# The last token tile of each PEER layer from gathered expert rows in place of dense products

## The reference

```python
def peer_ffn(h, wq, k1, k2, u, v):
    q = (ht @ wq).reshape(n_tok, 8, 256)
    s1 = einsum('thd,kd->thk', q[..., :128], k1)
    s2 = einsum('thd,kd->thk', q[..., 128:], k2)
    t1, i1 = top_k(s1, 16)
    t2, i2 = top_k(s2, 16)
    cand_s = t1[..., :, None] + t2[..., None, :]      # 256 candidates a head
    cand_i = i1[..., :, None] * 128 + i2[..., None, :]
    top_s, pos = top_k(cand_s, 16)
    idx = take_along_axis(cand_i, pos)
    g = softmax(top_s)
    act = gelu(einsum('td,thkd->thk', h, u[idx]))
    return einsum('thk,thkd->td', g * act, v[idx])
```

## Time and profile before

| | |
|---|---|
| median of 3 runs | 5623.86 us |
| the profiled execution, its own time | 5619.01 us |
| its span | 5617.2 us |
| mean granted clock of TensorE | 0.925 of 2.4 GHz |
| choosing, layer 0 / layer 1 | 1152 / 850 us |
| combining, layer 0 / layer 1 | 1034 / 690 us |
| DMA traffic | 751 MB, mean 134 GB/s |

### The profile page before, as it was taken

One profiled execution on the slowest core, in us unless ns is written; L12 is line 12 of the kernel. 1 busy time (PEld: TensorE's weight loads), 2 busy tenths in 40 slices (PEclk: granted clock), 3 DMA queues, 4 the chain that ended last, 5 costly groups with the idle time before them and its releaser, 6 DMA issues. The chain is left out here.

```text
span 5617.2 us, 76254 instructions
## 1 busy us (share of the span) xinstructions
PE 4840.5 (86%) x25386; PEld 2520.6 (45%) x25386; DVE 3699.3 (66%) x8384; ACT 1489.9 (27%) x1771; POOL 1637.2 (29%) x700
## 2 busy tenths in 40 slices
PE   9687754789999999989999994776888898799996
PEld 1244543456556555634444442333444444344443
DVE  0213334429999999567777675683388998288886
ACT  0002222013333333322222220461133333232331
POOL 0220000432222222233333332322433332344543
PEclk9898776899999999999999996887999999999998
DMA  8200001133544455454453530102335545665553
GB/s 352 90 30 10 5 2 59 35 99 114 169 155 138 145 169 162 158 195 186 150 187 150 187 149 30 64 30 84 123 124 185 167 151 157 211 214 198 198 202 120
DMA packets 395773, 751.43 MB, mean 134 GB/s; under 512 B 26436, under 2 KB 211588, under 8 KB 391428
## 3 DMA queue, kind: packets, MB, share of 16 engines
q1 hardware_dynamic: 170792, 556.03, 27.9%
q10 hardware_dynamic: 224864, 194.07, 10.9%
HBM read 569.55 MB, written 180.45 MB: 134 GB/s over the span
## 5 line engine op out<-in xcount | busy, mean ns | idle before, releaser
L1476 PE MATMUL ex_R<-ex_vh,ex_wh 128*128 128x512 f16 x2560 | 971.7, 380 | 52.0 <-DVE ex_wl L1491 52.0
L1214 PE MATMUL ca_A<-hh,ca_uh 128*128 128x512 f16 (+1 forms) x3072 | 902.6, 348 | 117.6 <-POOL ca_ul L1203 117.5
L1203 POOL TENSOR_TENSOR ca_ul<-ca_ur,ca_uh 128x1024 f16<-128x1024 f32 x256 | 563.1, 2200 | 1468.0 <-ACT ca_uh L1245 1468.0
L1476 PE MATMUL ex_R<-ex_vl,ex_wh 128*128 128x512 f16 x2560 | 971.6, 380 | 0.0
L1476 PE MATMUL ex_R<-ex_vh,ex_wl 128*128 128x512 f16 x2560 | 971.5, 379 | 0.0
L1451 POOL TENSOR_TENSOR ex_vl<-ex_vr,ex_vh 128x1024 f16<-128x1024 f32 x256 | 661.0, 2608 | 988.8 <-ACT ex_vh L1460 988.8
L1214 PE MATMUL ca_A<-hl,ca_uh 128*128 128x512 f16 (+1 forms) x3072 | 901.3, 348 | 0.0
L1214 PE MATMUL ca_A<-hh,ca_ul 128*128 128x512 f16 (+1 forms) x3072 | 899.3, 347 | 0.0
L1499 DVE TENSOR_TENSOR ACC<-ACC,ex_R 128x512 f32<-128x512 f32 x640 | 408.2, 678 | 402.9 <-PE ex_R L1476 402.9
L1487 DVE TENSOR_TENSOR ex_ar<-ex_ar,ex_gr 128x768 f32<-128x768 f32 (+1 forms) x256 | 498.1, 2002 | 185.5 <-DMA ex_ar<-acts 184.7
L1460 ACT ACTIVATE ex_vh<-ex_vr 128x1024 f16<-128x1024 f32 x256 | 267.5, 1045 | 1040.3 <-PE ex_R L1476 994.1
(11 more groups left out here) (306 smaller groups left out, 5835.5 us busy)
## 6 DMA issues: line engine op xcount, KB each, us to landing
ca_ur<-in_peer_u SPq DMA_DIRECT2D x256, 512.0 KB, 3.5
ex_vr<-in_peer_v SPq DMA_DIRECT2D x256, 512.0 KB, 6.9
gates<-ca_stage ACTq DMA_DIRECT2D x40, 2048.0 KB, 10.4
mod_w<-in_mod_w SPq DMA_DIRECT2D x12, 4096.0 KB, 12.4
acts<-ca_ga ACTq DMA_DIRECT2D x128, 384.0 KB, 2.3
ex_gr<-gates SPq DMA_DIRECT2D x128, 384.0 KB, 7.1
ex_ar<-acts SPq DMA_DIRECT2D x128, 384.0 KB, 7.6
acts<-ca_ga ACTq DMA_DIRECT2D x128, 256.0 KB, 2.8
```

The costliest lines, as they stand in the source:

```text
L1203: nc.gpsimd.tensor_tensor(ul[j][:, :, :], ur[j][:, :, :], uh[j][:, :, :], ALU.subtract).then_inc(u_cut, 1)
L1214: last = nc.tensor.matmul(A[b][:, a:a + w], lhs[b][:, k, :], rhs[:, k, a:a + w], start=(k == 0 and x == 0), stop=(k == KD - 1 and x == 2))
L1476: last = nc.tensor.matmul(R[(NP * q + y) % BANKS][:, :], lhs[q][:, x, o:o + P], rhs[q][:, x, h * 512:h * 512 + 512], start=(x == 0 and n = ...
```

## The change

The dense products leave out the last tile of each layer (`NT` is one tile shorter). For that tile:

- In `choose_and_activate` the choices are still made, as a last `choices(nt, True)` without gates behind it; the expert numbers go to `chosen_rows` and the softmax weights to `chosen_gates`, [128 tokens, 128] each. `ahead` and `beside` change. A few buffers are merged.
- In `combine_experts` each group of four chunks also treats SLOTS = 4 of the 128 picks of every token. POOL gathers with an indirect DMA, for each of the 128 partitions, one row of u, and later one of v (4 KB a partition, 512 KB a gather). DVE forms the dot product of the u row with the token's own input (`hp`, kept in PSUM), with an accumulator output; ACT applies the GELU to four numbers; DVE multiplies with the gates and adds share x v row to `sum_ps` in PSUM. The slots of group g stand on DVE between the weights of group g+1 and the adds of group g, and sum the v rows of group g-1. The number of PSUM banks for the pieces falls from 8 to 4.
- POOL's order in a group: the four low parts of v, a wait for the next index, four u gathers, each behind its dot product, four v gathers, each behind its sum.
- `project_and_norm` writes the modulated rows of the last tile to `HS`, which lives on, in place of `tmp`.

```diff
-    NT = TOK - c0
+    NT = TOK - c0 - P
...
-    ahead, beside = (8, 6) if nt == TILES else (12, 8)
+    ahead, beside = (12, 6) if nt == TILES - 1 else (20, 10)
     CT = ahead + TURNS * beside
...
+                begin(nt - 1)
                 gates_of(nt - 1)
                 for x in range(tail):
                     if x % 2 == 0 and x // 2 < PARTS:
                         store(nt - 1, x // 2)
                     chunk((CT * nt + x) // 2, x % 2)
+                    if x == tail // 2:
+                        midway(nt)
...
+                        if gathered:
+                            nc.vector.tensor_copy(chosen_rows[:, :], pick.rearrange("p h k -> p (h k)"))
...
-                        step(nc.vector.tensor_tensor(sel[:, 2, :, :], ex[:, :, :], sm[:, :, 1:2].broadcast_to([P, PH, PTOP]), ALU.mult))
+                        shares = chosen_gates[:, :].rearrange("p (h k) -> p h k", h=PH) if gathered else sel[:, 2, :, :]
+                        step(nc.vector.tensor_tensor(shares, ex[:, :, :], sm[:, :, 1:2].broadcast_to([P, PH, PTOP]), ALU.mult))
...
                     gates_of(nt - 1)
+                    choices(nt, True)
...
-    pieces = [(t, h) for t in range(first_tile, TILES) for h in range(2)]
+    pieces = [(t, h) for t in range(first_tile, TILES - 1) for h in range(2)]
     NP = len(pieces)
-    BANKS = 8
+    BANKS = 4
+    SLOTS = PH * PTOP // NG
...
                 @block.gpsimd
                 def _(pool):
+                    def gather(rows, ring, x, q, done):
+                        pool.sem_inc(issuing, 1)
+                        nc.gpsimd.indirect_dma_start(ring[x][:, :], None, rows,
+                                                     bass.IndirectOffsetOnAxis(ap=index[q][:, x:x + 1], axis=0)).then_inc(done[x], 16)
+
+                    def low(it, q, x):
+                        pool.wait_ge(v_high, it * (2 * GC) + GC * q + (x + 1))
+                        pool.wait_ge(second_done, it * (2 * NP) + NP * (q + 1))
+                        nc.gpsimd.tensor_tensor(vl[q][:, x, :], vr[x][:, :], vh[q][:, x, :], ALU.subtract).then_inc(v_cut, 1)
+
                     pool.sem_inc(v_cut, 4)
...
+                    pool.wait_ge(index_set, 1)
+                    for x in range(SLOTS):
+                        gather(u_rows, ug, x, 0, ug_in)
+
+                    def group(it, q, following):
+                        for x in range(GC):
+                            low(it, q, x)
+                        if following:
+                            pool.wait_ge(index_set, it * 2 + (q + 2))
+                            for x in range(SLOTS):
+                                pool.wait_ge(dotted, it * (2 * SLOTS) + (SLOTS * q + x + 1))
+                                gather(u_rows, ug, x, 1 - q, ug_in)
+                        for x in range(SLOTS):
+                            pool.wait_ge(summed, it * (2 * SLOTS) + (SLOTS * q + x + 1))
+                            gather(v_rows, vg, x, q, vg_in)
...
                 @block.scalar
                 def _(act):
...
+                    casts(0, 0)
+                    with act.Fori(0, NG // 2 - 1) as it:
+                        casts(it * 2 + 1, 1)
+                        gelu(it * 2, 0)
+                        casts(it * 2 + 2, 0)
+                        gelu(it * 2 + 1, 1)
...
                 @block.vector
...
+                    def slots(g, q, first=False, last=False):
+
+                        if not first:
+                            dve.wait_ge(gelu_done, g)
+                            nc.vector.tensor_tensor(share[1 - q][:, :], dot[1 - q][:, :], chosen_gates[:, bass.ds(g * SLOTS - SLOTS, SLOTS)],
+                                                    ALU.mult).then_inc(shared, 1)
+                            dve.wait_ge(shared, g)
+                        for x in range(SLOTS):
+                            if not last:
+                                dve.wait_ge(ug_in[x], g * 16 + 16)
+                                nc.vector.scalar_tensor_tensor(ug[x][:, :], ug[x][:, :], 1.0, hp[:, :], ALU.mult, ALU.mult,
+                                                               accum_out=dot[q][:, x:x + 1]).then_inc(dotted, 1)
+                            if first:
+                                dve.sem_inc(summed, 1)
+                            else:
+                                dve.wait_ge(vg_in[x], g * 16)
+                                dve.wait_ge(summed, g * SLOTS + x)
+                                nc.vector.scalar_tensor_tensor(sum_ps[:, :], vg[x][:, :], share[1 - q][:, x:x + 1], sum_ps[:, :],
+                                                               ALU.mult, ALU.add).then_inc(summed, 1)
+                        if not last:
+                            set_index(g + 1, 1 - q, g == NG - 1 if isinstance(g, int) else False)
...
                     with dve.Fori(0, NG // 2 - 1) as it:
-                        weights(it * 2 + 1, 1)
-                        add(it * 2, 0)
                         weights(it * 2 + 2, 0)
+                        slots(it * 2 + 1, 1)
                         add(it * 2 + 1, 1)
+                        weights(it * 2 + 3, 1)
+                        slots(it * 2 + 2, 0)
+                        add(it * 2 + 2, 0)
```

More of the change, by code:

```diff
@@ L826, in project_and_norm @@
     if after:
-        hh, hl, ident, next_layer, shift = after
+        hh, hl, ident, next_layer, shift, HS = after
+        rows_of = lambda i: HS if HS is not None and i == n - 1 else tmp[i % 2]
     o_gate = (layer * N_MOD + 2 + 3 * which) * D
@@ L1077, with choose_and_activate @@
 CAND = sum((a1 - a0) * nb for a0, a1, nb in RECTS)
-def choose_and_activate(nc, io, ident, hh, hl, scores, gates, acts, layer, first_tile):
+def choose_and_activate(nc, io, ident, hh, hl, scores, gates, acts, chosen_rows, chosen_gates, layer, first_tile):
     c0 = first_tile * P
-    NT = TOK - c0
+    NT = TOK - c0 - P
     nt = NT // P
@@ new lines, in _, with casts @@
+                    nc.scalar.activation(hp[:, :], HS[:, :], ACT.Copy).then_inc(rows_ready, 1)
+                    def casts(g, q):
+                        act.wait_ge(second_done, g * NP + NP)
+                        for x in range(GC):
+                            act.wait_ge(v_in[x], g * 16 + 16)
+                            nc.scalar.activation(vh[q][:, x, :], vr[x][:, :], ACT.Copy).then_inc(v_high, 1)
+                            act.wait_ge(weighed, g * GC + (x + 1))
+                            nc.scalar.activation(wh[q][:, x, :], ar[x][:, :], ACT.Copy).then_inc(w_high, 1)
@@ new lines, in gelu @@
+                    def gelu(g, q):
+                        act.wait_ge(dotted, g * SLOTS + SLOTS)
+                        nc.scalar.activation(dot[q][:, :], dot[q][:, :], ACT.Gelu).then_inc(gelu_done, 1)
+                    casts(0, 0)
[4 more added lines that the diff above has]
+                        gelu(it * 2 + 1, 1)
+                    casts(NG - 1, 1)
@@ L1505, in _ @@
-                    dve.wait_ge(cleared, 1)
+                    nc.vector.memset(sum_ps[:, :], 0.0).then_inc(cleared, 1)
+                    nc.vector.memset(ACC[:, first_tile:TILES - 1, :], 0.0).then_inc(cleared, 1)
+                    dve.wait_ge(cleared, 2)
+                    dve.wait_ge(rows_ready, 2)
+                    weights(1, 1)
+                    slots(0, 0, first=True)
+                    add(0, 0)
                     with dve.Fori(0, NG // 2 - 1) as it:
-                        weights(it * 2 + 1, 1)
-                        add(it * 2, 0)
@@ L1509, in _ @@
                         weights(it * 2 + 2, 0)
+                        slots(it * 2 + 1, 1)
                         add(it * 2 + 1, 1)
-                    weights(NG - 1, 1)
-                    add(NG - 2, 0)
+                        weights(it * 2 + 3, 1)
+                        slots(it * 2 + 2, 0)
+                        add(it * 2 + 2, 0)
+                    slots(NG - 1, 1)
                     add(NG - 1, 1)
+                    slots(NG, 0, last=True)
 def decay_rates(nc, io, rates):
@@ L1849, in more_inputs @@
     give("peer_v", a["peer_v"].reshape(DEPTH, PCH, P, D))
+    for layer in range(DEPTH):
+        give(f"peer_u_rows{layer}", a["peer_u"][layer])
+        give(f"peer_v_rows{layer}", a["peer_v"][layer])
     w = a["od_w_in"][0].reshape(KD, P, 2, RG_N, P)
```

106 lines of the change are left out of this document (61 added, 45 removed).

## The result

The change makes the kernel slower: 6175.8 us median (6174.7 to 6182.6) against 5622.7 (5620.1 to 5626.3), a ratio of 1.0986 with a 95% interval of 1.0973 to 1.1. The profiled execution took 6174.65 us, with a span of 6172.9 us against 5617.2.

What follows compares the result with a forecast made beforehand. PE was taken as the bound of combining, PE and VectorE as balanced in choosing; after the change POOL's queue order decides combining. Choosing -279, combining +234 and +550, copies +5 give +510 on 5624: 6135 us, range 5760 to 6650.

Steps and rivals of the forecast that it cites:

- the loop through POOL's queue: Combining: passes, eight gathers, four low parts, v load, casts and weights in series; 38.4 and 37.9 us a group.
- choosing: Expert-choosing stages, both layers: narrower products save 135 us in layer 0 and 144 in layer 1, -279 together.
- combining: Expert-combining stages, both layers: a longer group costs +234 us in layer 0 and +550 in layer 1.
- the bank loop: Layer 0 combining: with four PSUM banks PE stands during weights and passes; 33.8 to 36.4 us a group, close below.
- two distant bounds: POOL's time per gather: between a 0.34 us hardware-queue DMA issue and a 2.12 us POOL pass; middle 1.25 us taken.
- rival B: Combining: gathers nearly free at 0.34 us, landing 4.5 us, layer 1 at 28.2 us a group; total 5715; 13%.
- 82 us: Layer 0 choosing, choices phase: 12 chunks of PE at 6.5 us plus some 4 us of lag.
- 94 us: Layer 1 choosing, choices phase: 20 chunks at 4.2 us plus 10 us for POOL's waits for VectorE.
- my 10 us a tile: Layer 1 choosing: allowance added to each choices phase because POOL at times waits for VectorE.
- D: Combining: added work dearer, gathers of 3 us (7025 us) or VectorE passes of 2.18 us (about 6630); 13%.
- C: Whole kernel faster: choosing's 279 us outrun combining's loss, layer 1 under 26.4 us a group; 5585 us; 4%.
- E: Combining: PE stays the bound and 330 us are saved there too; 5015 us; under 1%.

Runs made afterwards that it cites:

- e1: The changed kernel with the next group's index copy moved ahead of VectorE's eight passes; 5942.9 us.
- e3: The changed kernel with the four v gathers of each group left out and all passes kept; 5931.2 us.
- e4: The changed kernel with every gather kept but bringing 1 KB a row in place of 4 KB; 6150.4 us.
- e5: The changed kernel with VectorE's two passes per gathered row replaced by their counts, gathers and index copies kept; 5672.9 us.
- e8: The changed kernel with fewer choosing chunks ahead of the turn and more beside the gates (8 and 8 in layer 0, 16 and 12 in layer 1); 6098.4 us.
- e7: The changed kernel with POOL's next low parts ahead of the gathers, as in e2, and each pass placed behind one add; 5465.7 us.
- e9: e7 with the index copy ahead of the passes, POOL waiting for the weights before its low parts, and gathers in the order of the passes; 5380.3 us.
- e10: e9 with the chunk counts of e8; 5291.6 us median of four runs, a ratio of 0.9419 to the kernel before the change.
- e2: The changed kernel with POOL doing the next group's four low parts ahead of the gathers; 6107.5 us.

## Why the prediction was right

The forecast was 6135 us, 0.7% under the 6176 measured, by the mechanism that e1, e3, e4 and e5 confirm: the time of a group is the loop through POOL's queue. Two terms were off, choosing by 107 us and combining by 62 the other way; that they partly cancelled is luck, and without it the 0.7% would have been 1 to 2%.

*Combining*, +784 forecast, +722 measured. The loop's terms for layer 1: the passes 10.4 forecast, 9.6 measured (the accumulator's read is 0.08 us); a gather 1.25, measured 1.245; low parts 8.5, measured 8.35; landing of v with the casts and weights behind it 9.0, measured 8.25; and a hand-off of 1.0 us from the index copy to the first gather that I had left out. 37.9 became 36.9. The rest of that term is its base: I set 20.7 us against it, but layer 1's stage before was 690/32 = 21.6 us a group, start and end included. In layer 0 38.4 stood against 38.9 measured. There the two loops lie close together: e1 shows that the bank loop takes over at 35.9, inside the 33.8 to 36.4 that I gave it.

The gather, the price that no row showed, was the middle of two distant bounds and came out right by luck as much as by reason; what carried the forecast is that both bounds gave a slower kernel. By the Trainium skill's figure of about 1 us ("DMA: Bandwidth & Descriptors", "Latency and other measured facts") the sum would have been 6007, by the prediction's estimate. The row shows 0.94 us for the instruction, close to it; but from start to start, which is what a queue of eight pays, it is 1.245.

Of what the next profile was to show, the period, the low parts right behind the gathers and VectorE's wait ahead of `ex_ar` came as forecast. PE's share did not: 72% and 55% of the two combining stages, for 67% and 41%, since the same matmuls took longer at granted clocks of 0.86 and 0.75 (0.28 us each in layer 1, 0.217 before). And a sign that was named for rival B did show, adds that wait for PE in layer 1; it said nothing for B, because that wait is covered.

*Choosing*, -279 forecast, -172 measured, is the step that failed: "82 us" and "94 us" for the phase ahead of the turn were 91.2 and 111.5, from these rows of VectorE (the choices start at 1442.47 and 4410.54, the turn is copied here):

```profile
1533.69 0.56 DVE L1380 COPY ca_cols<-ca_G 128x384 f32<-128x384 f32 x1 [29.60 <-PE ca_G L1227]
...
4522.02 0.56 DVE L1380 COPY ca_cols<-ca_G 128x384 f32<-128x384 f32 x1 [45.77 <-PE ca_G L1227]
```

of POOL in the same phases, layer 0 and then layer 1:

```profile
1478.78 5.56 POOL L1207 TENSOR_TENSOR ca_ul<-ca_ur,ca_uh 128x1024 f16<-128x1024 f32 x1 [0.71 <-ACT ca_uh L1249]
1496.03 2.12 POOL L1207 TENSOR_TENSOR ca_ul<-ca_ur,ca_uh 128x1024 f16<-128x1024 f32 x1 [11.70 <-ACT ca_uh L1249]
...
4428.83 2.13 POOL L1207 TENSOR_TENSOR ca_ul<-ca_ur,ca_uh 128x1024 f16<-128x1024 f32 x1 [1.49 <-ACT ca_uh L1249]
4437.74 2.13 POOL L1207 TENSOR_TENSOR ca_ul<-ca_ur,ca_uh 128x1024 f16<-128x1024 f32 x1 [1.47 <-ACT ca_uh L1249]
...
4498.39 2.12 POOL L1207 TENSOR_TENSOR ca_ul<-ca_ur,ca_uh 128x1024 f16<-128x1024 f32 x1 [1.38 <-ACT ca_uh L1249]
...
4508.61 2.14 POOL L1207 TENSOR_TENSOR ca_ul<-ca_ur,ca_uh 128x1024 f16<-128x1024 f32 x1 [1.38 <-ACT ca_uh L1249]
```

and of ScalarE (ACTq is its issue of a store):

```profile
1487.15 6.19 ACTq L1279 DMA_DIRECT2D gates<-ca_stage  x1
1493.61 1.28 ACT L1249 ACT_TABLE_LOAD   x1 [5.06 <-issue]
...
4502.69 1.28 ACT L1249 ACT_TABLE_LOAD   x1 [0.95 <-ACT ca_ga L1256]
```

In layer 0 twelve chunks at PE's 6.5 us and 4 us of lag are the 82 us, and PE's waits for a low part of u add 8.8 us in this phase. Two low parts of 5.5 us beside VectorE's two-source passes make 1.9 of it. The other 6.9 are one wait: ScalarE does the tile's exponential, the issue of a gates store takes it 6.19 us where 0.39 is usual, it loads an activation table (1.28 us) before the next cast and again before the next GELU, and POOL sits idle for 11.7 us behind that. The trace of the kernel before has this wait too (PE waits 6.0 us once between 1422 and 1495 us), and the prediction has no term for it. Five such phases, 8 to 11 us each, less 1 to 3 us on each gates phase, are the 40 us by which 1057 exceeds 1017.

In layer 1 a pair of chunks takes 8.9 us early in the phase (4428.83 to 4437.74), 4.5 a chunk where I had 4.2. The exponential and its store then cost some 8 us, of which my 10 us a tile, meant for POOL's slow low parts, held nothing. Behind it each pair takes 10.22 us (4498.39 to 4508.61): the two table loads of 1.28 us now stand in every second chunk, and one of them lies in the loop of PE, GELU, cast, low part and PE (10.22 less 1.28 is 8.94). An estimate from these rows is 5 us for the slower chunks, 8 for the exponential and 5 for the table loads, about the 17.5 us by which the phase exceeds 94; no run took one of them away. Three phases of that and gates phases of 120 to 123 us instead of 118 make 773 out of 706. e8 shows the other side: with fewer chunks ahead, half the wait is recovered.

The rivals. B (gathers nearly free) falls with the 1.245 us. D falls: a gather takes nowhere near 3 us and a dot product 1.22, not 2.18. C (faster) asked for a loop under 26.4 us in layer 1 and was nowhere near with this order of POOL's queue; but e7, e9 and e10 are faster, by taking the loop apart rather than by cheaper parts. E said that nothing in the diff lets passes and low parts run beside each other. That is true of the diff; e7 does it by accident and e9 by one wait.

## What to carry to other kernels

When work moves to an engine that is 29% busy, write out its queue for one period and mark what each instruction waits for: here the eight gathers could start only after the last pass, and four instructions that were there before stood behind them, with the next loads behind those. Such a loop is not cured by cheaper parts (gathers of a quarter of the bytes gained 25 us) but by order: releasing the gathers by pass, putting the low parts before them, and spreading the adds among the passes turned, with a rebalanced choosing stage, a loss of 9.8% into a gain of 5.8% with the same number of instructions on PE, VectorE and POOL. And each reordering must be checked for what then runs side by side: the same early index copy gained 233 us in one version and cost 285 in another.

## What the runs showed of the hardware that I had not expected

- An indirect DMA of 128 rows occupies GpSimd for 0.94 us whether a row has 1 KB or 4 KB, and eight of them follow each other at 1.245 us.
- Next to VectorE's weights passes in e7 the same instruction takes longer: 1.15 us in the median and up to 1.45 for the u gathers, which stand there, against 0.94 for the v gathers, most of which come later.
- Four low halves of the weights (128x384, both inputs in SBUF) took 10.64 us beside GpSimd's low parts in e2, where one alone takes 0.56, while GpSimd's own four took 8.37 there and 8.35 without them. In layer 0 of e2 both were slower, GpSimd's four at 10.14.
- ScalarE loads an activation table in 1.28 us. In layer 1's choosing two such loads stand in each pair of chunks behind the tile's exponential and none ahead of it.
- With DMA engines 85 to 89% busy a whole combining stage ran at 325 to 327 GB/s, against 213 to 226 with the change's order and the same gathers. So the rate in the change's trace was no limit of the transfers; the waits set it.
- A running sum kept in PSUM as both input and output (128x1024, f32) takes 1.28 us, where the dot product over the same row takes 1.22 with 0.08 us for its accumulator.
- PE's granted clock in layer 1's combining fell to 0.75 with PE busy 55% of the time, and stood at 0.86 in e10 at 73%: I read this as the clock following the pauses; no run held the clock and changed the pauses alone, so it stays a reading.
